# Eight weight slots from the last part of the output projection on, with its adds and the norm's parameter loads reordered

## The chip, the cores and the metric

One core of one Trainium2 chip. The metric is the device time of one execution, in microseconds; a number given for a kernel is the median of several runs. A profiled execution gives the span from the first instruction to the last and the trace that rows are read from.

## The reference

Two post-norm residual layers over an input x of (1, 256, 2048) in float32; each layer is a mixer and an MLP, and each of these ends in a layer norm:

```python
for l in range(DEPTH):                                   # DEPTH = 2
    if l % 2 == 0:   # input projection 2048 -> 6144, conformer convolution + HGRN2 recurrence
        mix = jnp.concatenate([a_out, b_out], axis=-1) @ ev_w_out[j]
    else:            # input projection 2048 -> 6152, forgetting attention + chunked attention
        mix = jnp.concatenate([c_out, d_out], axis=-1) @ od_w_out[j]
    x = layer_norm(ALPHA * x + mix, ln_mix_g[l], ln_mix_b[l])
    h = jnp.square(jax.nn.relu(x @ mlp_w1[l])) @ mlp_w2[l]      # 2048 -> 8192 -> 2048
    x = layer_norm(ALPHA * x + h, ln_mlp_g[l], ln_mlp_b[l])
```

layer_norm subtracts the row's mean, divides by the root of its variance, and multiplies by g and adds b, vectors of 2048. So there are four norms: behind mixer 0, MLP 0, mixer 1 and MLP 1.

## The kernel before, in words

All products are fp32 products made of three fp32r matmuls. Every weight value is split into a high and a low part, and so is every activation: high times high, weight-low times high, weight-high times activation-low (L1303, L1304, L1305).

**Slots.** Weights stream through in chunks of 256 rows by 512 columns, 512 KB each, numbered 0 to 767 over the whole program; the number is called the slot. Layer 0's mixer has slots 0 to 127 (0 to 95 its input projection, 96 to 127 its output projection), MLP 0 has 128 to 383, layer 1's mixer 384 to 511 and MLP 1 512 to 767. For each slot s there are four steps on four engines:

- SP loads the chunk into `raw`, a ring of 4 buffers, once the split of slot s - 4 is done (L314, L341 in the MLP).
- ScalarE copies it rounded into `w_hi` (the split; L476, L702 in the MLP) and increments `hi_ready`.
- VectorE subtracts that from raw into `w_lo` (L788, L1176 in the MLP) and increments `lo_ready`.
- TensorE does 12 matmuls with it, 6 for each half of the 256 rows of x (r = 0 and r = 1), and increments `chunk_used` at the end of r = 1.

`w_hi` and `w_lo` have 4 buffers each in the mixers, and 8 in the MLPs, where the other four (`w_hi2`, `w_lo2`) lie in scratch memory `scr` that the mixers use for their own intermediates. `deep(s)` says where eight are used: slots 128 to 391, and from 512 on. `used_before(s)` is the slot whose buffer s takes, and so the slot that TensorE must be done with before s is split: s - 4 or s - 8. The first four slots of each MLP (128 to 131, 512 to 515) wait for none, since nothing used their buffers.

**Tiles.** A tile is 512 output columns for 256 rows, in one of two PSUM buffers (`gemm0`, `gemm1`); tile t needs the buffer of t - 2 emptied. The output projection goes by three parts of its input (groups of channels as they become ready), each with four tiles; the last part has slots 120 to 127 in layer 0 and 504 to 511 in layer 1, two slots to a tile, tiles 20 to 23. Tile 19 is the last of the part before. VectorE adds each tile to the residual X, once for each half of the rows (`add_row`, L816). For the last part it takes the row statistics at once (`tile_stats`, L831). Where the add of a tile stands among the splits on VectorE is set by `add_before(s)`: ahead of the split of the slot four after the tile's last one. The last two tiles (22, 23) are done rows first: TensorE does r = 0 of slots 124 to 127, then r = 1 of them.

**The norm.** `mix_norm` first runs VectorE's splits up to slot 131 (515), then `layer_norm` with `first_rows`, the adds of tiles 22 and 23 for r = 0, then mean and variance (L840, L842), subtraction of the mean times g (`centre`, L846), a reciprocal root on POOL (`inverse_root`, L404), scaling plus b (`scale`, L852). TensorE transposes the normed pieces (`row_piece`, L1415), the first piece already in the middle of the last slot of tile 23; ScalarE and VectorE make `x_hi` (`row_hi`, L501) and `x_lo` (`row_lo`, L863) of them. `second_rows` are the adds for r = 1. Splits of slots 132 to 139 stand among these steps, by `upto` in `layer_norm` on ScalarE and on VectorE. The norm behind MLP 0 runs by the same function, with only one tile left to add.

**The MLP.** Four blocks of 32 + 32 slots: four tiles with w1, four with w2. After a w1 tile ScalarE does relu (L696) and square (L698, `h_row`), and TensorE transposes the result (`hidden`, L1689) behind the first four half-slots of the next tile. On ScalarE relu and square of tile i stand behind the splits of the first seven slots of the next tile, so for the first tile of an MLP behind those of slots 140, 141 and 142 (524, 525, 526).

**POOL.** It has one stream of instructions. It loads the norm's g and b, each spread to all 128 partitions, into the two rows of `lnp` (`ln_params`, L369), as soon as the last norm's scaling is done, and behind the second such load the constants of the odd layer (`odd_constants`). For the first norm it waits for the transposes of the last recurrence output (`pair_full`, O1) and for `cat_ready`, since `lnp` held the convolution's and the recurrence's rows.

## Time and profile before

| what | value |
|---|---|
| median of 3 runs | 2310.24 us (2310.06 to 2310.41) |
| the profiled execution | 2308.35 us, span 2306.6 us |
| TensorE matmuls busy | 2250.6 us (98%) |
| VectorE busy | 1342.0 us (58%) |
| ScalarE busy | 1056.7 us (46%) |
| POOL busy | 35.8 us (2%) |
| mean granted TensorE clock | 0.991 |
| read from HBM | 414.79 MB, 181 GB/s over the span with what is written |
| each load of a weight chunk / of a row of norm parameters | 512 KB / 1024 KB |

Matmuls are pipelined, so that their busy time overlaps; a stretch in which TensorE waits shows in the waits and in gaps of its timeline, not in the 98%. The granted clock is given as a share of 2.4 GHz. A landing time is from a load's issue to the arrival of its data.

### The profile page before, as it was taken

To read this page: it belongs to the slowest core of one execution; us is meant where nothing else is said; L and a number is where in the kernel's file an instruction comes from. 1 tells how busy PE (TensorE), PEld (TensorE's weight loads), DVE (VectorE), ACT (ScalarE), POOL (GpSimd) and SP (SyncE) were. 2 spreads that over 40 slices of the span, in tenths; PEclk is the share of its full clock that TensorE was granted. 3 is DMA by queue.
4 is the path that set the end of the run, shared out by engine and by line. 5 is a ranking of instruction groups with operands and counts; after the bars stand their busy time and mean duration, and the time that the engine had idled before them with its cause. 6 is when DMAs were issued, how large, how long until landed. Compare 5 with 4: busy or idle time off the path is not lost.

```text
span 2306.6 us, 28499 instructions
## 1 busy us (share of the span) xinstructions
PE 2250.6 (98%) x10331; PEld 1865.2 (81%) x10331; DVE 1342.0 (58%) x1472; ACT 1056.7 (46%) x1146; POOL 35.8 (2%) x68
## 2 busy tenths in 40 slices
PE   8999999889999999999999999998999999999998
PEld 7888788668888888888878888886888888888886
DVE  4898986845544445544565545567454445454455
ACT  4555565344444344344434444444444444543542
POOL 2000000000000000000000000000000000000000
PEclk9999999989999999999999999999999999999999
DMA  7555535575655555655545555565556555556553
GB/s 241 167 161 156 173 128 170 178 225 183 192 191 188 196 183 182 199 193 183 191 163 157 170 177 165 168 192 193 186 186 200 183 197 183 182 193 200 183 188 109
DMA packets 213040, 418.50 MB, mean 181 GB/s; under 512 B 12793, under 2 KB 13361, under 8 KB 211904
## 3 DMA queue, kind: packets, MB, share of 16 engines
q1 hardware_dynamic: 211120, 406.90, 55.0%
q0 software_dynamic: 1808, 10.04, 1.2%
q8 instruction: 78, 1.28, 0.2%
q14 instruction: 34, 0.28, 0.0%
HBM read 414.79 MB, written 2.10 MB: 181 GB/s over the span
## 4 chain that ended last, share of the span: by engine, by line
PE 90%; DVE 5%; DMA 2%; issue 1%; ACT 1%; DVEq 0%; SPq 0%; ACTq 0%
PE gemm L1303 28%; PE gemm L1305 28%; PE gemm L1304 28%; DVE lnp L1047 2%; DMA raw<-in_mlp_w 2%; PE pair L1689 1%; DVE w_lo L788 1%; PE pair L1458 1%; ACT w_hi L476 1%; PE pair L1375 1%; PE pair L1415 1%; DVE X L846 0%; PE pair L1531 0%; PE pair L1603 0%; PE pair L1576 0%
## 5 line engine op out<-in xcount | busy, mean ns | idle before, releaser
L1176 DVE TENSOR_TENSOR w_lo<-raw,w_hi 128x1024 fp32r<-128x1024 f32 x488 | 596.7, 1225 | 491.4 <-ACT w_hi L702 459.7
L702 ACT ACTIVATE w_hi<-raw 128x1024 fp32r<-128x1024 f32 x492 | 522.1, 1061 | 646.5 <-PE gemm L1305 625.2
L1303 PE MATMUL gemm<-w_hi,x_hi 128*128 128x512 f32 x1792 | 711.3, 397 | 7.9 <-DVE w_lo L788 7.6
L1305 PE MATMUL gemm<-w_hi,x_lo 128*128 128x512 f32 x1792 | 701.0, 391 | 0.0
L1304 PE MATMUL gemm<-w_lo,x_hi 128*128 128x512 f32 x1792 | 700.6, 391 | 0.0
L1303 PE MATMUL gemm<-w_hi,c_hi 128*128 128x512 f32 x1280 | 501.2, 392 | 1.0 <-DVE X L813 1.0
L1304 PE MATMUL gemm<-w_lo,c_hi 128*128 128x512 f32 x1280 | 499.0, 390 | 0.0
L1305 PE MATMUL gemm<-w_hi,c_lo 128*128 128x512 f32 x1280 | 499.0, 390 | 0.0
L788 DVE TENSOR_TENSOR w_lo<-raw,w_hi 128x1024 fp32r<-128x1024 f32 x280 | 340.3, 1222 | 205.1 <-ACT w_hi L476 199.6
L476 ACT ACTIVATE w_hi<-raw 128x1024 fp32r<-128x1024 f32 x276 | 289.4, 1056 | 304.6 <-PE gemm L1305 266.1
L1303 PEld LDWEIGHTS gemm<-w_hi,x_hi 128*128 128x128 f32 x1792 | 338.5, 189 | 83.1 <-issue 6.7
L1305 PEld LDWEIGHTS gemm<-w_hi,x_lo 128*128 128x128 f32 x1792 | 338.2, 189 | 71.7
L1304 PEld LDWEIGHTS gemm<-w_lo,x_hi 128*128 128x128 f32 x1792 | 338.7, 189 | 67.0
L1303 PEld LDWEIGHTS gemm<-w_hi,c_hi 128*128 128x128 f32 x1280 | 241.1, 188 | 50.5 <-DVE X L813 1.2
L1305 PEld LDWEIGHTS gemm<-w_hi,c_lo 128*128 128x128 f32 x1280 | 240.9, 188 | 49.9
L1304 PEld LDWEIGHTS gemm<-w_lo,c_hi 128*128 128x128 f32 x1280 | 240.9, 188 | 49.5
L1148 DVE SCALAR_TENSOR_TENSOR X<-X,factor,gemm 128x512 f32<-128x512 f32 x64 | 47.6, 744 | 109.0 <-PE gemm L1305 109.0
L1047 DVE SCALAR_TENSOR_TENSOR lnp<-scr,lnp 128x256 f32<-128x256 f32 x240 | 100.4, 479 | 0.0
L1161 DVE TENSOR_TENSOR c_lo<-pair,c_hi 128x1024 fp32r<-128x1024 f32 x32 | 39.2, 1225 | 92.3 <-ACT c_hi L689 92.2
L689 ACT ACTIVATE c_hi<-pair 128x1024 fp32r<-128x1024 f32 x32 | 32.9, 1027 | 99.0 <-PE pair L1689 99.0
L1689 PE MATMUL pair<-ident,scr 128*128 128x128 f32 x256 | 34.1, 277 | 14.8 <-ACT scr L698 14.8
L1689 PEld LDWEIGHTS pair<-ident,scr 128*128 128x128 f32 x256 | 30.6, 144 | 19.6 <-ACT scr L698 15.6
(194 smaller groups left out, 784.2 us busy)
## 6 DMA issues: line engine op xcount, KB each, us to landing
raw<-in_mlp_w SPq DMA_DIRECT2D x512, 512.0 KB, 4.7
raw<-in_ev_w_in SPq DMA_DIRECT2D x96, 512.0 KB, 3.8
raw<-in_od_w_in SPq DMA_DIRECT2D x96, 512.0 KB, 4.0
raw<-in_ev_w_out SPq DMA_DIRECT2D x32, 512.0 KB, 4.0
raw<-in_od_w_out SPq DMA_DIRECT2D x32, 512.0 KB, 3.6
lnp<-in_ln_mix_g POOLq DMA_DIRECT2D x2, 1024.0 KB, 5.8
lnp<-in_ln_mix_b POOLq DMA_DIRECT2D x2, 1024.0 KB, 8.0
lnp<-in_ln_mlp_g POOLq DMA_DIRECT2D x2, 1024.0 KB, 5.2
```

Of the source, the lines that this page charges most:

```text
L476: act.activation(hi_of_chunk(s), raw[:, s % RING], ACT.Copy).then_inc(hi_ready, 1)
L689: act.activation(c_hi[:, 4 * (i - 1):4 * i, :], quad[0], ACT.Copy).then_inc(h_hi, 1)
L702: act.activation(hi_of_chunk(s), raw[:, s % RING], ACT.Copy).then_inc(hi_ready, 1)
L788: dve.tensor_tensor(lo_of_chunk(s), raw[:, s % RING], hi_of_chunk(s).bitcast(F32), ALU.subtract).then_inc(lo_ready, 1)
L1047: ins = dve.scalar_tensor_tensor(out=cv[:, ch, :], in0=src, scalar=cw[:, ch, j:j + 1], in1=cv[:, ch, :], op0=ALU.mult, op1=ALU.add)
L1148: dve.scalar_tensor_tensor(out=Xj, in0=Xj, scalar=factor[:, bass.ds(b, 1)], in1=gemm[t % 2][:, r, :], op0=ALU.mult, op1=ALU.add).then_inc( ...
L1161: dve.tensor_tensor(c_lo[:, 4 * (i - 1):4 * i, :], quad[0], c_hi[:, 4 * (i - 1):4 * i, :].bitcast(F32), ALU.subtract).then_inc(h_ready, 1)
L1176: dve.tensor_tensor(lo_of_chunk(s), raw[:, s % RING], hi_of_chunk(s).bitcast(F32), ALU.subtract).then_inc(lo_ready, 1)
L1303: pe.matmul(acc[:, r, :], hi[:, k + c, rows], high, start=begin, stop=False)
L1304: pe.matmul(acc[:, r, :], hi[:, k + c, rows], low, start=False, stop=False)
L1305: return pe.matmul(acc[:, r, :], lo[:, k + c, rows], high, start=False, stop=end)
L1689: ins = pe.transpose(quad[0][:, cc, r * P:(r + 1) * P], urow[(i - 1) % 2][:, r, cc * P:(cc + 1) * P], ident[:, :])
```

## The change

- `deep`, `used_before`: eight slots from the first slot of the last part (120 and 504, the new list `DEEP0`) on. The first four of them, whose buffers lie in scratch memory, wait for slot 111 (495) to be done, the end of the mixer's use of that memory (`SCR_FREE`). Slots 128 to 131 (512 to 515) now wait for the slot eight before.
- `add_before`: from tile 19 on an add stands ahead of the split eight after the tile's last slot.
- `second_rows` now has three steps, and `add_row` can leave its statistics to `row_stats`. In VectorE's `layer_norm` the first of them stands ahead of the scaling and the second ahead of the first `row_lo`; the third piece is scaled behind the second `row_lo`.
- ScalarE's `layer_norm`: one more split ahead of the first `row_hi`, and one more ahead of the third.
- POOL: g for the first norm as soon as the convolution is done with its row of `lnp`, b behind O1. Parameters of later norms wait for `h_row` 8 (24) in the second block of the MLP or, for the norm of mixer 1, for `chunk_used` 400; the odd constants for `h_row` 12, in the third block.

TensorE's and SP's instructions keep their order.

```diff
--- before.py
+++ after.py
@@ -95,9 +95,15 @@
 STORES = [(0, 0, 8), (0, 8, 8), (1, 0, 4), (1, 4, 4), (1, 8, 4), (1, 12, 4)]
 
 
+
+
+DEEP0 = [SLOT_MLP[layer] - DEEP for layer in range(DEPTH)]
+SCR_FREE = [SLOT0[layer] + LEVEL_SLOT[1] + 22 for layer in range(DEPTH)]
+
+
 def deep(s):
 
-    return SLOT_MLP[0] <= s < SLOT0[1] + CPT or s >= SLOT_MLP[1]
+    return DEEP0[0] <= s < SLOT0[1] + CPT or s >= DEEP0[1]
 
 
 def slot_of(s):
@@ -106,8 +112,11 @@
 
 def used_before(s):
 
+    for layer in range(DEPTH):
+        if s in range(DEEP0[layer], DEEP0[layer] + RING):
+            return SCR_FREE[layer] - 1
     if deep(s):
-        return None if s in range(SLOT_MLP[0], SLOT_MLP[0] + RING) or s in range(SLOT_MLP[1], SLOT_MLP[1] + RING) else s - DEEP
+        return s - DEEP
     return s - RING if s >= RING else None
 
 
@@ -445,15 +454,23 @@
 
                 pool.tensor_tensor(ss, ss, mhalf[:, 0:8], ALU.pow).then_inc(rstd_ready, 1)
 
+
+            pool.wait_ge(conv_ready, 1)
+            row(lnp[:, 0, :], ln_mix_g[0], D, lnp_loaded)
             pool.wait_ge(pair_full[0], USE[0]["O1"] + 1)
-            pool.wait_ge(cat_ready, 2)
-            ln_params(0)
+            row(lnp[:, 1, :], ln_mix_b[0], D, lnp_loaded)
 
             inverse_root(1)
             for which in range(1, 4):
                 pool.wait_ge(normed, NO * which)
+
+                if which == 2:
+                    pool.wait_ge(chunk_used, SLOT0[1] + 2 * CPT)
+                else:
+                    pool.wait_ge(h_row, FB * NT * (which // 2) + 2 * NT)
                 ln_params(which)
                 if which == 1:
+                    pool.wait_ge(h_row, 3 * NT)
                     odd_constants()
                 inverse_root(1 + which)
 
@@ -504,14 +521,11 @@
             def layer_norm(which, s0, ahead):
 
 
-                upto(s0 + 5)
-                for n in (0, 1, 2):
-                    row_hi(which, n)
                 upto(s0 + 6)
-                row_hi(which, 3)
-                row_hi(which, 4)
+                row_hi(which, 0)
+                row_hi(which, 1)
                 upto(s0 + 7)
-                for n in (5, 6, 7):
+                for n in range(2, 8):
                     row_hi(which, n)
                 upto(s0 + CPT - 1 + min(ahead, 1))
                 row_hi(which, 8)
@@ -799,7 +813,7 @@
                 dve.wait_ge(hi_sem, value)
                 dve.tensor_tensor(lo, quad[p][:, 0:lo.shape[1], :], hi.bitcast(F32), ALU.subtract).then_inc(ready, 1)
 
-            def add_row(layer, part, j, r):
+            def add_row(layer, part, j, r, with_stats=True):
 
                 i = 12 + NT * part + j
                 t = TILE0[layer] + i
@@ -814,16 +828,20 @@
                                              ).then_inc(done, 1)
                 else:
                     dve.tensor_tensor(Xj, tile, Xj, ALU.add).then_inc(done, 1)
-                if part == PARTS - 1:
-                    dve.wait_ge(done, NT * ((PARTS + FB) * layer + part) + j + 1)
-                    tile_stats(j, r)
+                if part == PARTS - 1 and with_stats:
+                    row_stats(layer, j, r)
+
+            def row_stats(layer, j, r):
+                dve.wait_ge((x_sum0, x_sum)[r], NT * ((PARTS + FB) * layer + PARTS - 1) + j + 1)
+                tile_stats(j, r)
 
             def add_before(s):
 
                 for layer in range(DEPTH):
                     for part in range(PARTS):
                         for j in range(NT if part < PARTS - 1 else NT - 2):
-                            if s == SLOT0[layer] + PART_SLOT[part] + PART_CHUNKS[part] * (j + 1) - 1 + RING:
+                            last = SLOT0[layer] + PART_SLOT[part] + PART_CHUNKS[part] * (j + 1) - 1
+                            if s == (last + RING if last + RING < DEEP0[layer] else last + DEEP):
                                 for r in range(RT):
                                     add_row(layer, part, j, r)
 
@@ -870,13 +888,15 @@
                 dve.wait_ge(lnp_loaded, 32 * which)
                 statistics(which, 0, taken)
                 c = [centre(0, *PIECES[i]) for i in range(3)]
+                second_rows[0]()
                 rstd_wait(which, 0)
-                for i in range(3):
-                    scale(0, *PIECES[i], c[i])
+                scale(0, *PIECES[0], c[0])
+                scale(0, *PIECES[1], c[1])
+                second_rows[1]()
                 row_lo(which, 0)
-                second_rows[0]()
                 row_lo(which, 1)
-                second_rows[1]()
+                scale(0, *PIECES[2], c[2])
+                second_rows[2]()
                 row_lo(which, 2)
                 statistics(which, 1, RT * NT)
                 c = [centre(1, *PIECES[i]) for i in range(3)]
@@ -911,8 +931,8 @@
                 rstd_wait(4, 0)
                 for piece, centred in zip(STORES[:2], c):
                     scale(*piece, centred)
-                second_rows[0]()
-                second_rows[1]()
+                for rows in second_rows:
+                    rows()
                 statistics(4, 1, RT * NT)
                 c = [centre(*piece) for piece in STORES[2:]]
                 rstd_wait(4, 1)
@@ -1128,12 +1148,15 @@
             def mix_norm(layer):
                 upto(SLOT_MLP[layer] + RING - 1)
                 x_sums[0] += PARTS * NT
+                part = PARTS - 1
 
                 def first_rows():
-                    add_row(layer, PARTS - 1, NT - 2, 0)
-                    add_row(layer, PARTS - 1, NT - 1, 0)
-
-                second_rows = [lambda: add_row(layer, PARTS - 1, NT - 2, 1), lambda: add_row(layer, PARTS - 1, NT - 1, 1)]
+                    add_row(layer, part, NT - 2, 0)
+                    add_row(layer, part, NT - 1, 0)
+
+                second_rows = [lambda: add_row(layer, part, NT - 2, 1, with_stats=False),
+                               lambda: row_stats(layer, NT - 2, 1),
+                               lambda: add_row(layer, part, NT - 1, 1)]
                 layer_norm(2 * layer + 1, SLOT_MLP[layer], first_rows, second_rows, RT * NT - 2, RING)
 
             def add_block(layer, b, j, r):
@@ -1190,7 +1213,7 @@
                 def first_rows():
                     add_last(layer, NT - 1, 0)
 
-                second_rows = [lambda: None, lambda: add_last(layer, NT - 1, 1)]
+                second_rows = [lambda: None, lambda: None, lambda: add_last(layer, NT - 1, 1)]
                 if layer == 0:
                     upto(SLOT0[1] + RING - 1)
                     layer_norm(2, SLOT0[1], first_rows, second_rows, RT * NT - 1, 0)
```

VectorE from the split of slot 509 to the norm of mixer 1, before (`w_lo2` is the second set of four buffers; `rows_done` counts tiles whose r = 0 is done, `x_sum0` and `x_sum` the adds for r = 0 and r = 1):

```order
L788 TENSOR_TENSOR w_lo<-raw,w_hi 128x1024 [waits chunk_used,raw_full2,hi_ready]
L816 TENSOR_TENSOR X<-gemm1,X 128x512 [waits rows_done]
L831 BN_STATS stats<-X 128x6 [waits x_sum0]
L816 TENSOR_TENSOR X<-gemm1,X 128x512 [waits chunk_used]
L831 BN_STATS stats<-X 128x6 [waits x_sum]
L788 TENSOR_TENSOR w_lo<-raw,w_hi 128x1024 [waits chunk_used,raw_full3,hi_ready]
L788 TENSOR_TENSOR w_lo2<-raw,w_hi2 128x1024 [waits raw_full0,hi_ready]
L788 TENSOR_TENSOR w_lo2<-raw,w_hi2 128x1024 [waits raw_full1,hi_ready]
L788 TENSOR_TENSOR w_lo2<-raw,w_hi2 128x1024 [waits raw_full2,hi_ready]
L788 TENSOR_TENSOR w_lo2<-raw,w_hi2 128x1024 [waits raw_full3,hi_ready]
L816 TENSOR_TENSOR X<-gemm0,X 128x512 [waits rows_done]
L831 BN_STATS stats<-X 128x6 [waits x_sum0]
```

The same stretch now, from the split of slot 510 on:

```order
L802 TENSOR_TENSOR w_lo<-raw,w_hi 128x1024 [waits chunk_used,raw_full2,hi_ready]
L830 TENSOR_TENSOR X<-gemm1,X 128x512 [waits rows_done]
L830 TENSOR_TENSOR X<-gemm1,X 128x512 [waits chunk_used]
L802 TENSOR_TENSOR w_lo<-raw,w_hi 128x1024 [waits chunk_used,raw_full3,hi_ready]
L802 TENSOR_TENSOR w_lo2<-raw,w_hi2 128x1024 [waits chunk_used,raw_full0,hi_ready]
L830 TENSOR_TENSOR X<-gemm0,X 128x512 [waits rows_done]
L849 BN_STATS stats<-X 128x6 [waits x_sum0]
L830 TENSOR_TENSOR X<-gemm0,X 128x512 [waits chunk_used]
L849 BN_STATS stats<-X 128x6 [waits x_sum]
L802 TENSOR_TENSOR w_lo2<-raw,w_hi2 128x1024 [waits chunk_used,raw_full1,hi_ready]
L802 TENSOR_TENSOR w_lo2<-raw,w_hi2 128x1024 [waits chunk_used,raw_full2,hi_ready]
```

The add of tile 19 stands behind the split of 510 instead of 506, that of tile 20 behind 512 and that of tile 21 (not shown) behind 514; the split of 515 then is the only one between it and the adds of tiles 22 and 23.

VectorE at the scaling of the norm of mixer 1, from the add for r = 1 that now stands ahead of it:

```order
L830 TENSOR_TENSOR X<-gemm0,X 128x512 [waits chunk_used]
L870 SCALAR_TENSOR_TENSOR X<-X,rstd,lnp 128x256 [waits dve_link,rstd_ready]
L870 SCALAR_TENSOR_TENSOR X<-X,rstd,lnp 128x256 [waits dve_link]
L849 BN_STATS stats<-X 128x6 [waits x_sum]
L881 TENSOR_TENSOR x_lo<-pair0,x_hi 128x2x128 [waits xt_hi]
L881 TENSOR_TENSOR x_lo<-pair1,x_hi 128x2x128 [waits xt_hi]
L870 SCALAR_TENSOR_TENSOR X<-X,rstd,lnp 128x512 [waits dve_link]
L830 TENSOR_TENSOR X<-gemm1,X 128x512 [waits chunk_used]
```

Before, three scalings stood first, then the first `x_lo`, the add of tile 22 with its statistics, the second `x_lo`, and the add of tile 23.

## Rows read from the trace of the kernel before

**Rows 1.** Who TensorE waited for: total us, times, longest us.
```profile
PE pair L1689 <- ACT scr L698: 14.8, 2, 10.7
PE pair L1415 <- DVE X L852: 11.7, 5, 5.7
```
**Rows 2.** Timeline, TensorE: start us, us, engine, line, operation [idle before <- releaser].
```profile
432.08 0.66 PE L1415 MATMUL pair<-ident,X 128*128 128x128 f32 x2 [5.72 <-DVE X L852]
...
479.49 1.97 PE L1689 MATMUL pair<-ident,scr 128*128 128x128 f32 x8 [10.71 <-ACT scr L698]
...
1165.09 0.38 PE L1415 MATMUL pair<-ident,X 128*128 128x128 f32 x2
...
1189.02 0.30 PE L1415 MATMUL pair<-ident,X 128*128 128x128 f32 x1 [0.35 <-DVE X L852]
...
1569.20 0.66 PE L1415 MATMUL pair<-ident,X 128*128 128x128 f32 x2 [4.84 <-DVE X L852]
...
1594.81 0.30 PE L1415 MATMUL pair<-ident,X 128*128 128x128 f32 x1 [0.39 <-DVE X L852]
...
1609.74 0.33 PE L1689 MATMUL pair<-ident,scr 128*128 128x128 f32 x1 [4.06 <-ACT scr L698]
```
**Rows 3.** Stretches: length, busy us (instructions) of each engine, PEclk, DMA share, GB/s.
```profile
264.00:272.00 8.00, 4.59 (x24) 3.55 (x24) 8.00 (x17) 2.54 (x3) 0.00 (x0) 1.00 0.27 74
...
479.50:485.00 5.50, 5.50 (x18) 4.74 (x19) 2.45 (x2) 2.79 (x3) 0.00 (x0) 0.54 0.80 260
1609.70:1615.00 5.30, 5.26 (x20) 4.34 (x21) 3.06 (x3) 3.02 (x3) 0.00 (x0) 0.68 0.87 281
```
**Rows 4.** Timeline, VectorE, ahead of the norm of mixer 1.
```profile
1556.43 4.62 DVE L788 TENSOR_TENSOR w_lo<-raw,w_hi 128x1024 fp32r<-128x1024 f32 x4
...
1563.92 0.68 DVE L816 TENSOR_TENSOR X<-gemm,X 128x512 f32<-128x512 f32 x1
...
1565.25 0.67 DVE L816 TENSOR_TENSOR X<-gemm,X 128x512 f32<-128x512 f32 x1
...
1568.58 1.54 DVE L852 SCALAR_TENSOR_TENSOR X<-X,rstd,lnp 128x256 f32<-128x256 f32 x3
```
**Rows 5.** Landing times of weight loads (L341) issued from 440 to 458.5.
```profile
DMA to landing us min/median/max: 3.8/4.1/4.3
```
**Rows 6.** Timeline, ScalarE, splits of slots 121, 125 and 126.
```profile
400.78 1.05 ACT L476 ACTIVATE w_hi<-raw 128x1024 fp32r<-128x1024 f32 x1
...
410.82 1.06 ACT L476 ACTIVATE w_hi<-raw 128x1024 fp32r<-128x1024 f32 x1 [1.66 <-PE gemm L1305]
413.54 1.06 ACT L476 ACTIVATE w_hi<-raw 128x1024 fp32r<-128x1024 f32 x1 [1.66 <-PE gemm L1305]
```
**Rows 7.** Timeline, SP's queue: issue of the loads for slots 125 and 526.
```profile
403.31 0.37 SPq L314 DMA_DIRECT2D raw<-in_ev_w_out  x1
...
1599.23 0.37 SPq L341 DMA_DIRECT2D raw<-in_mlp_w  x1
```
**Rows 8.** Landing times of weight loads (L314) issued from 400 to 412.
```profile
DMA to landing us min/median/max: 5.5/6.9/7.3
```
**Rows 9.** Timeline, POOL: first of the two parameter loads, two norms.
```profile
1189.17 0.61 POOL L369 DMA_DIRECT2D lnp<-in_ln_mix_g  x1 [18.13 <-DVE X L852]
...
1594.96 0.58 POOL L369 DMA_DIRECT2D lnp<-in_ln_mlp_g  x1 [18.15 <-DVE X L852]
```
**Rows 10.** Landing times of weight loads (L341) issued from 1596 to 1603.
```profile
DMA to landing us min/median/max: 7.2/7.5/7.9
```
**Rows 11.** Landing times of weight loads (L341) issued from 458.5 to 470.
```profile
DMA to landing us min/median/max: 11.8/13.9/14.3
```
**Rows 12.** Timeline, ScalarE: split of slot 526, then square.
```profile
1606.63 1.06 ACT L702 ACTIVATE w_hi<-raw 128x1024 fp32r<-128x1024 f32 x1 [0.30 <-DMA raw<-in_mlp_w]
...
1608.63 1.06 ACT L698 ACTIVATE scr<-scr 128x1024 f32<-128x1024 f32 x1
```
**Rows 13.** ScalarE's waits for DMA in the MLPs: total us, times, longest us.
```profile
ACT w_hi L702 <- DMA raw<-in_mlp_w: 21.2, 6, 10.4
```

## The prediction

> **What bounds the kernel now.** I read the views from the total down to single rows. The waits of TensorE come first [rows 1]: it idles for 26.5 us at two lines, 14.8 us at the transposes of the hidden rows (L1689) and 11.7 us at the transposes of freshly normed rows (L1415). The timeline of TensorE says where [rows 2]. Four waits make 25.3 us: 5.72 and 4.84 us before the first transposes behind the mixer's norm (432.08 in layer 0, 1569.20 in layer 1), and 10.71 and 4.06 us before the first hidden transposes of each MLP (479.49, 1609.74). The norm behind the first MLP, at 1165.09, waits for nothing, so it is the measure of an undisturbed norm. Everywhere else the matmuls are back to back and nothing on another engine counts.
>
> A wait costs more than itself. The granted clock was 0.54 in 479.5 to 485.0 and 0.68 in 1609.7 to 1615.0 [rows 3], so part of these stretches ran at 1.2 GHz instead of 2.4 after TensorE had idled 10.71 and 4.06 us: (1 - 0.54) x 5.5 = 2.5 us and (1 - 0.68) x 5.3 = 1.7 us lost. Behind the norms the loss is read from lengths: from first to last front transposes the undisturbed norm takes 1189.02 - 1165.09 = 23.93 us, layer 1's takes 1594.81 - 1569.20 = 25.61 us: 1.7 us lost; I take 1.7 for layer 0 too. In 264 to 272, with 8.00 - 4.59 = 3.41 us of idleness in it, the clock stayed at 1.00 [rows 3]: shorter waits lose none. All four places together hold 25.3 + 7.6 = 32.9 us.
>
> **Wait 1, the mixer's norm.** What ends last is VectorE. In layer 1 it did four splits from 1556.43 (the next MLP's first slots), the last of them late, and began the adds of the last tiles at 1563.92 [rows 4], when TensorE had long finished the first rows of these tiles. From the add at 1565.25 to TensorE's restart at 1569.20 are 3.95 us. Layer 0 has the same order.
>
> With eight slots from the last part on, splits 120 to 131 no longer wait for the slot four back but for the one eight back, so the four splits stand ahead of the adds in time, not behind. Costs on VectorE: a split 4.62 / 4 = 1.15 us, an add with its statistics 1565.25 - 1563.92 = 1.33, both halves 2.66.
>
> Layer 1: ScalarE's splits there waited for TensorE, not for DMA. Loads land in 3.8 to 4.3 us when quiet [rows 5], and a buffer of four comes round in 4.1 + 1.06 + 1.15 plus hand-overs, 6.5 us, 1.6 per slot against 2.72 per slot of TensorE (from one released split to the next) [rows 6]. Starting with split 504, VectorE gains about 1.1 us per slot and reaches the add of tile 19 (now behind split 510) some 2 us before TensorE asks for it. The last four slots run as 5.44 us of first rows, then second rows. First rows of the last tile end 4.7 us before 1564.4, at 1559.7; VectorE is through split 515 and the add before by then. From there 3.95 + 0.65 (the add of the second rows, put in ahead of the scaling) gives 1564.3: TensorE stands there at 1564.36. Wait gone, clock kept; of the new order behind it, 0.3 us may show since the statistics come ahead of the first x_lo. Gain 4.84 + 1.7 - 0.3 = **6.2**.
>
> Layer 0: the ramp starts later, since ScalarE is held by the c_hi copy until its split 121 at 400.78 [rows 6]. The load for slot 125 went out at 403.31 [rows 7] and does so again. Loads between 400 and 412 landed in 5.5 to 7.3 us beside 2 MB of norm parameters [rows 8]; 1 MB of these is now earlier, so I take 5, and 3.8 and 7.3 as ends. Slot 125 lands at 408.3, 126 by 409.5, split 126 ends at 411.6, and the add of tile 19, which stands behind it now, ends at 412.9. TensorE wants tile 21's buffer at 410.8 (the end of slot 121, which released the split at 410.82): **a new wait of 2.1 us** (ends 0.9 and 4.4). What is queued on VectorE behind it: splits 127 to 131 (5 x 1.13 back to back), two tiles' adds (5.3), the first add of the last tiles (1.33), then 4.6: 16.9 us, restart at 429.8. TensorE's own work from 412.9 is 5.44 + 5.44 + 4.7 = 15.6, so it waits again, 1.3 us. Restart 429.8 against 432.08 is 2.3, plus the clock 1.7: **4.0**.
>
> **Wait 2, the first hidden transposes.** The norm parameters leave POOL's queue at 1594.96 [rows 9], just when SP starts on the slots that the norm held back [rows 7]. Between 1596 and 1603 these landed in 7.2 to 7.9 us [rows 10]; in layer 0, where odd-layer constants followed, in 11.8 to 14.3 [rows 11], against 3.8 to 4.3 just before [rows 5]. The square that TensorE waits for stands on ScalarE behind three of these splits: split 1606.63, square ending 3.1 us later [rows 12]. With the parameters gone, the third load, issued at 1599.23, lands at about 4.5 us, 1603.8, and the square is done at 1606.9; TensorE wants it at 1609.74 - 4.06 = 1605.68. **1.2 us stay** (4.1 to 4.9 us of landing give 0.8 to 1.6), short enough to keep the clock. Layer 1 gains 4.06 - 1.2 + 1.7 = **4.5**, layer 0 10.71 - 1.2 + 2.5 = **12.0**.
>
> DMA: Bandwidth & Descriptors of the Trainium skill, section Issuing engines are not separate DMA queues, says that transfers issued from different engines run on the same DMA engines and interleave. By that rule, the trace agrees that POOL's loads delay SP's [rows 10, 11]. It also speaks against the change: bytes moved to another moment still interleave with weight loads there, and the sum would lose what they cost at the new place.
>
> **What moving the loads costs.** 2 MB go into the second block of each MLP, the constants into the third block of the first, 2 MB into layer 1 at slot 400, 1 MB to about 387 us. In the MLP, ScalarE waited for DMA at L702 six times, 21.2 us [rows 13], and all six lie behind the two mixer norms: in the middle it never did. A load issued there has four slots (10.9 us) less 2.3 us of splitting, 8.6, before ScalarE is late, and four more slots before TensorE is. 7.9 us fits, 14.3 is covered by the eight slots. At slot 400 only four slots exist: 8.6 us before ScalarE, some 14 before TensorE; 7.9 fits too, and 2 MB issued at 1189.17 [rows 9], some ten slots earlier, cost TensorE no wait. So 0, with bounds of 0 and 3. If that cover is gone, the price is Wait 2's, 12 us at worst.
>
> SP's order is unchanged; POOL's waits have only its own reciprocal roots behind them, which come due hundreds of us later. ScalarE's split 134 ahead of the first x_hi needs the slot done half a chunk before: 0 to 0.3. The norm at 1165 changes its order and has no wait to lose: 0 (bounds -0.3 and 0.3). The last norm is as before.
>
> **Sum.** 6.2 + 4.0 + 12.0 + 4.5 = 26.7 us off the profiled execution, 2308.35 (span 2306.6), which stands 1.9 below the median of the runs, 2310.24. So 2281.7 there, **2283.5** for the median. Bounds: all four waits and clock losses gone, 32.9: 2277.3. Least: layer 0's norm 1, layer 1's 4.5, the hidden waits 9.5 and 2.5, mid-stage -3: 14.5, 2295.7.
>
> **The rivals.**
> - *The hidden waits are the four raw buffers', not the parameters'.* Then layer 0 falls only to what layer 1 has, 4.06 + 1.7, a gain of 7.4, and layer 1 keeps its own. For: even by my sum the third load is late. Against: 7.2 to 7.9 us of landing. 10.2 + 7.4 = 17.6: 2292.6. Chance 0.12.
> - *VectorE stays the chain at the norm*: the ramp never gets ahead, as nearly in layer 0, and new waits eat the old. Only 16.5: 2293.7. Chance 0.11. In layer 0 alone: 2287.5, part of my range.
> - *The loads starve TensorE at their new places.* They share the DMA engines with the weight loads there too, and each of the three places costs what layer 0's now does [rows 2, 3], 10.71 + 2.5 = 13.2 us, 39.6 in all against 26.7 gained: 2323.1, slower. It decides from 8.9 us apiece; it needs landings beyond 14 us at all three. Against: no such wait in mid-stage now [rows 13]. Chance 0.02; a partial loss that ends between 2295 and 2305, 0.04.
> - *The change does not do what it says*: the eight slots wait for slot 111 at their start. It ended some 22 us before slot 120 begins (eight slots of 2.72), so it holds nobody. 2310, chance 0.02.
>
> **How the numbers follow.** My forecast has 0.69 and its own range is 2278 to 2290. Taking in the first two rivals leaves out under 0.2: 2277.5 to 2294. A measurement of this kernel tells 0.2% (4.6 us) from no change. Faster needs under 2305.6: 0.95; same 0.02; slower 0.03.
>
> **What would show it.** In the profile after: at the mixer norms L1415 waits under 0.5 us in layer 1 and 1 to 2 in layer 0, with a new wait of about 2 us for an add at about 411; L1689 waits about 1 us twice; ScalarE waits under 5 us for DMA at L702's successor in total; the granted clock stays 1.00 behind all four. Wrong if a hidden wait above 3 us stays, if TensorE idles at mid-MLP or near slot 400, or if the norm of layer 1 still waits over 2 us.

## The result, and the profile of the changed kernel

The changed kernel takes **2287.07 us** (median; 2285.41 to 2289.18) against 2310.32 for the kernel before, run beside it: a ratio of 0.9899, 95% interval 0.9882 to 0.9916. The forecast was 2283.5 in a range of 2277.5 to 2294.0. The profiled execution took 2288.11, a little over its median; before it was 2308.35, a little under, so the two profiles differ by 20.2 us and the medians by 23.2.

Who TensorE waited for, after: total us, times, longest us. These answer to [rows 1].
```profile
PE gemm L1326 <- DVE w_lo L802: 6.5, 8, 3.4
...
PE gemm L1326 <- DVE X L830: 3.4, 1, 3.4
PE pair L1712 <- ACT scr L712: 2.8, 2, 1.6
...
PE pair L1438 <- DVE X L870: 1.9, 4, 0.9
```
The transposes of normed rows (L1415 before, L1438 now) wait 1.9 us instead of 11.7, those of the hidden rows (L1689, now L1712) 2.8 instead of 14.8. One line is new: a matmul waits 3.4 us for an add. The first line holds waits for VectorE's splits, nearly all far from the change; the longest of them stands at 264 us, as before.

Timeline of TensorE after, the places that answer to [rows 2]; start us, us, engine, line, operation [idle before <- releaser].
```profile
414.92 0.79 PE L1326 MATMUL gemm<-w_hi,c_hi 128*128 128x512 f32 x1 [3.44 <-DVE X L830]
...
469.98 1.09 PE L1712 MATMUL pair<-ident,scr 128*128 128x128 f32 x8 [1.62 <-ACT scr L712]
...
1554.92 0.41 PE L1438 MATMUL pair<-ident,X 128*128 128x128 f32 x2 [0.85 <-DVE X L870]
...
1591.12 1.09 PE L1712 MATMUL pair<-ident,scr 128*128 128x128 f32 x8 [1.18 <-ACT scr L712]
```
Four waits again, but of 7.1 us instead of 25.3. The norm of layer 0 is not among them: nothing over 0.25 us is left ahead of its first transposes. In its place stands the new wait at 414.92, in front of slot 122, for the add of tile 19.

Stretches after, answering to [rows 3]: length, busy us (instructions) of PE, PEld, DVE, ACT, POOL, then the granted clock, DMA share, GB/s.
```profile
264.00:272.00 8.00, 4.63 (x13) 3.39 (x12) 8.00 (x18) 2.34 (x2) 0.00 (x0) 0.69 0.24 72
...
415.00:420.50 5.50, 5.50 (x13) 4.34 (x14) 5.43 (x7) 1.06 (x2) 0.00 (x0) 0.50 0.83 259
469.90:475.00 5.10, 5.02 (x26) 4.32 (x27) 3.67 (x3) 4.12 (x5) 0.00 (x0) 1.00 0.78 233
1273.00:1276.00 3.00, 3.00 (x10) 2.29 (x10) 0.00 (x0) 0.00 (x0) 0.00 (x0) 0.66 0.67 180
...
1554.90:1560.00 5.10, 5.03 (x24) 3.45 (x24) 4.46 (x9) 2.31 (x4) 0.00 (x0) 1.00 0.00 0
1591.00:1596.00 5.00, 4.88 (x26) 4.17 (x27) 3.65 (x3) 4.03 (x5) 0.00 (x0) 1.00 0.82 267
```
Behind the waits of 0.85 to 1.62 us the clock stays at 1.00, 2.4 GHz, in this profile. Behind the new wait it is 0.50, 1.2 GHz: the twelve matmuls of slot 122 take from 414.92 to the first of slot 123 at 420.21, 5.29 us for 2.72, so 2.6 us are lost beside the 3.44. The same happened in two places that the change does not touch: behind the wait at 264 (1.00 before, 0.69 now), and at 1274, where TensorE had not waited at all.

**Where the 20.2 us came from.** I took for each slot the start of its first matmul in the two profiles and noted how the difference steps. The mixer norm of layer 0, from slot 121 to slot 129, gave 1.15 us (old wait and clock gone, new wait and clock in); the hidden transposes behind it 11.5; the norm of layer 1 5.3; the hidden transposes of layer 1 4.5. That is 22.4. The other 2.2 went in code that the change does not touch: 1.4 by the clock at 1274 and 0.8 elsewhere, most of it behind the wait at 264, where the clock took 2.6 us and some 2 came back up to 306, where waits of the kernel before did not come. What is left is 20.2.

Layer 0's ramp after: ScalarE's splits of slots 125 to 127 (408.28, 411.35, 412.64), then VectorE with the splits of 125 and 126 and the two adds of tile 19.
```profile
408.28 1.06 ACT L493 ACTIVATE w_hi<-raw 128x1024 fp32r<-128x1024 f32 x1 [2.84 <-DMA raw<-in_ev_w_out]
411.35 1.06 ACT L493 ACTIVATE w_hi<-raw 128x1024 fp32r<-128x1024 f32 x1 [2.01 <-DMA raw<-in_ev_w_out]
412.64 1.06 ACT L493 ACTIVATE w_hi<-raw 128x1024 fp32r<-128x1024 f32 x1 [0.23 <-DMA raw<-in_ev_w_out]
```
```profile
409.37 1.23 DVE L802 TENSOR_TENSOR w_lo<-raw,w_hi 128x1024 fp32r<-128x1024 f32 x1 [1.92 <-ACT w_hi L493]
412.44 1.23 DVE L802 TENSOR_TENSOR w_lo<-raw,w_hi 128x1024 fp32r<-128x1024 f32 x1 [1.84 <-ACT w_hi L493]
413.58 1.28 DVE L830 TENSOR_TENSOR X<-gemm,X 128x512 f32<-128x512 f32 x2
```
In [rows 6] these splits waited for TensorE; now they wait for DMA: the load of slot 126 is what is late. TensorE wanted tile 21's buffer at 411.48, and the add that frees it could only follow split 126.

Landing times of weight loads after: issued 404 to 406.5; 460 to 472, behind layer 0's norm; 1570 to 1584, behind layer 1's. These answer to [rows 8], [rows 11] and [rows 10].
```profile
DMA to landing us min/median/max: 4.2/6.1/6.3
```
```profile
DMA to landing us min/median/max: 4.2/4.6/5.1
```
```profile
DMA to landing us min/median/max: 3.7/3.9/4.5
```
The loads ahead of the hidden transposes land in 4.6 us instead of 13.9, and in 3.9 instead of 7.5. Those of the ramp are better than before, but not quiet.

### The profile page after: what moved, and what is told of

Its sections match the earlier page's. It is cut to its first block, busy times and chain, and to the rows that moved or that the text cites. A ratio compares the mean times of both kernels' runs of the same rounds, so it can differ in the third digit from the quotient of the medians.

```text
span 2286.4 us, 28509 instructions
## 1 busy us (share of the span) xinstructions
PE 2249.9 (98%) x10331; PEld 1864.2 (82%) x10331; DVE 1341.9 (59%) x1472; ACT 1057.0 (46%) x1146; POOL 36.6 (2%) x68
## 3 DMA queue, kind: packets, MB, share of 16 engines
q8 instruction: 78, 1.28, 0.2%
## 4 chain that ended last, share of the span: by engine, by line
PE 91%; DVE 4%; DMA 2%; ACT 1%; issue 1%; DVEq 0%; SPq 0%; ACTq 0%
PE gemm L1326 29%; PE gemm L1328 29%; PE gemm L1327 29%; PE pair L1712 1%; DVE w_lo L802 1%; DVE lnp L1067 1%; DMA raw<-in_mlp_w 1%; PE pair L1481 1%; ACT w_hi L493 1%; PE pair L1398 1%; PE pair L1438 0%; PE pair L1554 0%; PE pair L1626 0%; PE pair L1599 0%; DVE X L864 0%
## 5 line engine op out<-in xcount | busy, mean ns | idle before, releaser
L710 ACT ACTIVATE scr<-gemm 128x1024 f32<-128x1024 f32 x32 | 32.9, 1028 | 8.1 <-PE gemm L1328 8.1
L1712 PEld LDWEIGHTS pair<-ident,scr 128*128 128x128 f32 x256 | 29.9, 141 | 7.6 <-ACT scr L712 3.6
```

Source lines behind the costliest of these rows:

```text
L1712: ins = pe.transpose(quad[0][:, cc, r * P:(r + 1) * P], urow[(i - 1) % 2][:, r, cc * P:(cc + 1) * P], ident[:, :])
```

## The experiments

**The theory to test.** The hidden waits went because the parameters left the DMA engines there; the loads cost nothing in mid-stage; what missed the forecast is one wait in layer 0, for the add of tile 19 behind a late load, and the clock behind it. **Rivals:** the ring of eight did most of it and the loads little; the loads at 387 and 401 us are themselves what delays the ramp; the new order inside the norms is what remains; and the extra loads in mid-stage take a little everywhere.

**1. The loads alone** (the kernel before with this edit and no other).
```diff
+            pool.wait_ge(conv_ready, 1)
+            row(lnp[:, 0, :], ln_mix_g[0], D, lnp_loaded)
...
-            pool.wait_ge(cat_ready, 2)
-            ln_params(0)
+            row(lnp[:, 1, :], ln_mix_b[0], D, lnp_loaded)
...
+                if which == 2:
+                    pool.wait_ge(chunk_used, SLOT0[1] + 2 * CPT)
+                else:
+                    pool.wait_ge(h_row, FB * NT * (which // 2) + 2 * NT)
...
+                    pool.wait_ge(h_row, 3 * NT)
```


> The kernel before with POOL's part of the change alone (parameter loads and constants in mid-stage). If the hidden waits were the parameters' and mid-stage is free, the two waits at the hidden transposes fall from 10.7 and 4.1 us to about 1.6 and 1.2, their clock loss goes, and the time falls by 15 to 17 us, to 2293 to 2296; both norm waits (5.7 and 4.8 us) stay. If the four raw buffers made the waits, 4 us stay at each and the gain is under 10 us. If the loads cost something at their new places, TensorE shows a wait in mid-MLP or near slot 400.

Measured 2293.25 us, ratio 0.993 (0.9913 to 0.9946): 16.4 us of the change's 23.2. Its four waits on TensorE:
```profile
431.15 0.42 PE L1422 MATMUL pair<-ident,X 128*128 128x128 f32 x2 [5.02 <-DVE X L859]
...
468.57 1.09 PE L1696 MATMUL pair<-ident,scr 128*128 128x128 f32 x8 [1.28 <-ACT scr L705]
...
1555.85 0.66 PE L1422 MATMUL pair<-ident,X 128*128 128x128 f32 x2 [4.80 <-DVE X L859]
...
1595.06 1.71 PE L1696 MATMUL pair<-ident,scr 128*128 128x128 f32 x8 [2.14 <-ACT scr L705]
```
The hidden waits fall from 10.71 and 4.06 to 1.28 and 2.14, and the norm waits stay. `raw` still has four buffers here, and the eight slots begin where they did. So most of the hidden waits was the parameters', which settles the first rival of the prediction.

**2. The ring and the order alone** (the changed kernel with the old place of POOL's loads, the edit of run 1 undone).

> The changed kernel with POOL's loads as before. If norms and loads are separate, the norm of layer 1 gains the same 5 to 6 us, and the hidden waits are back at 10 and 4 us. With 2 MB of parameters from 400 us on again, the loads for slots 125 and 126 land a us or two later than after the change, so the new wait for the add of tile 19 grows from 3.4 to 5 us or more and layer 0's norm loses. Time 2302 to 2306. If that wait has nothing to do with the parameters, it stays at 3.4 us.

Measured 2308.38 us, ratio 0.9996 (0.9986 to 1.0006): nothing gained that can be told from noise, and worse than expected. TensorE's waits, and the DMA page of the stretch 403 to 406.8 (queue: packets, MB, share of 16 engines; then KB and median us to landing):
```profile
417.11 0.79 PE L1319 MATMUL gemm<-w_hi,c_hi 128*128 128x512 f32 x1 [6.53 <-DVE X L823]
...
480.96 1.97 PE L1705 MATMUL pair<-ident,scr 128*128 128x128 f32 x8 [11.16 <-ACT scr L705]
...
1608.05 1.97 PE L1705 MATMUL pair<-ident,scr 128*128 128x128 f32 x8 [4.53 <-ACT scr L705]
```
```profile
q0 software_dynamic: 193, 1.43, 96.2%
...
raw<-in_ev_w_out SPq DMA_DIRECT2D x3, 512.0 KB, 9.2
```
With both parameter loads (POOL's queue, q0) in flight, the ramp's weight loads land in 9.2 us and the add of tile 19 is 6.53 us late, against 3.44. In layer 1, where no parameters are loaded in the ramp, the norm waits 1.14 us with 0.93 us for an add ahead of it, against 4.84 before, so the eight slots do gain there. The hidden waits and layer 0 ate it. By the medians the two halves are not additive: 16.4 and 1.2 us alone, 23.2 together. In layer 0 the eight slots need the loads gone from the ramp.

**3. The add of tile 19 two slots ahead, in both layers** (the changed kernel with this add before the split of 125 and 509, not behind 126 and 510).
```diff
-                            if s == (last + RING if last + RING < DEEP0[layer] else last + DEEP):
+                            if s == (last + RING if last + RING < DEEP0[layer] else last + DEEP - 2 * (part < PARTS - 1)):
```


> The changed kernel with the add of tile 19 two splits earlier (ahead of the split of slot 125 and 509). VectorE stood idle there for 1.9 us in layer 0. If the new wait is the order of VectorE, the 3.4 us at 411 and the low clock behind it (2.6 us) go, but VectorE's chain of splits and adds then ends later than TensorE, and a wait of 2 to 3.5 us comes back ahead of the first transposes at 427 to 430; net 3 us less than after the change. In layer 1 nothing changes. If the wait at 411 is the late loads themselves, it stays as a wait for the split of slot 122 or later.

Measured 2284.92 us, ratio 0.9901 (0.9884 to 0.9918). Its waits from 411 us to the norm of layer 0:
```profile
421.08 0.50 PE L1326 MATMUL gemm<-w_hi,c_hi 128*128 128x512 f32 x1 [1.87 <-DVE X L830]
429.99 0.41 PE L1438 MATMUL pair<-ident,X 128*128 128x128 f32 x2 [1.14 <-DVE X L870]
```
The wait of 3.44 is gone with its clock loss. Two come in its place further on, the second of them the one that the prediction had put there (1.3 us). Slot by slot this profile is 3 to 4 us ahead of the changed kernel's behind layer 0's norm; the medians show 2.2 of it, but the ratios to the kernel before, 0.9901 here and 0.9899 there, show nothing. So run 3 shows what made the wait, and not a gain in time.

**4. The second mixer parameter held until slot 121 is done.**
```diff
+            pool.wait_ge(chunk_used, SLOT_MLP[0] - 6)
             row(lnp[:, 1, :], ln_mix_b[0], D, lnp_loaded)
```


> The changed kernel with the load of b for the first norm held until slot 121 is done (411 us instead of 401). If that 1 MB delays the loads for slots 125 and 126, they land in about 4 us instead of 5 to 6, the split of 126 ends 2 us earlier and the wait for the add of tile 19 falls from 3.4 to about 1.5 us, with the clock kept: 4 us less in layer 0. If the loads were slow for another reason, the wait stays at 3.4.

Measured 2285.51 us, ratio 0.9898 (0.9881 to 0.9914). The wait, the landing of the loads issued from 403 to 406 (POOL's load now leaves at 411.15), and stretches of the ramp, columns as above:
```profile
414.20 0.63 PE L1327 MATMUL gemm<-w_hi,c_hi 128*128 128x512 f32 x1 [3.62 <-DVE X L831]
```
```profile
DMA to landing us min/median/max: 4.1/6.3/6.5
```
```profile
407.00:409.00 2.00, 2.00 (x10) 1.66 (x9) 0.60 (x1) 1.06 (x1) 0.00 (x0) 1.00 0.89 305
409.00:411.00 2.00, 1.58 (x7) 0.96 (x6) 0.62 (x1) 0.36 (x1) 0.00 (x0) 1.00 0.95 347
```
The wait stays, so the parameter is not its cause. The first of four loads issued 1.1 to 1.4 us apart lands in 4.1 us, the others in 6.3 to 6.5 (the fourth, in 6.4, is a load of the MLP and not in this view), with the DMA engines busy for 0.89 to 0.95 of the time. That fits loads that delay each other; no run spaced them out to show it. The quiet 3.8 to 4.3 us of [rows 5] were read where loads go out a slot apart. The clock was not kept behind this wait either: 0.70 in 414.3 to 420.

**5. As run 3, with relu and square one split earlier** in each MLP's first tile.
```diff
-                    if i < NT and c == CPT - 1:
+                    if i < NT and c == (CPT - 2 if i == 0 and CPT not in splits and RING in splits and 0 not in splits else CPT - 1):
```


> The kernel with the earlier add (e3) and, for the first tile of each MLP, relu and square one split earlier on ScalarE (ahead of slots 142 and 526, not behind). If the rest of the hidden waits (1.7 and 1.4 us) is the third weight load that relu stands behind, both vanish and nothing else moves: 3 us less than e3, about 2282. If ScalarE's split then comes too late for TensorE, a wait for w_lo takes their place.

Measured **2281.21 us**, ratio 0.9875 (0.986 to 0.989). No hidden wait over 0.25 us is left in layer 0, and 0.29 in layer 1. So the rest of the hidden waits was the third split that stood ahead of the square. The gain over run 3 and over the changed kernel is at the edge of the noise (the changed kernel's interval began at 0.9882); runs 10 and 11 come back to it.

**6. The old order inside the norms**, all else as changed.
```diff
+                upto(s0 + 5)
+                for n in (0, 1, 2):
+                    row_hi(which, n)
...
-                second_rows[0]()
                 rstd_wait(which, 0)
-                scale(0, *PIECES[0], c[0])
-                scale(0, *PIECES[1], c[1])
-                second_rows[1]()
+                for i in range(3):
+                    scale(0, *PIECES[i], c[i])
                 row_lo(which, 0)
+                second_rows[0]()
...
```


> The changed kernel with VectorE's and ScalarE's order inside the norms as before the change. The add for r = 1 no longer stands between the subtraction and the scaling, so TensorE restarts 0.65 us sooner at the norm of layer 1 (its wait of 0.85 us falls to 0.2 or so); behind it the adds and statistics delay the second and third x_lo, for which I expect new waits of 0.5 to 1.5 us in the first two slots. Net between -0.5 and +1.5 us per mixer norm: if the reorder was worth anything the time rises, by 2 us at most; the norm behind MLP 0 does not move.

Measured 2285.21 us, ratio 0.989 (0.9875 to 0.9906), the changed kernel's own within the intervals. Layer 1's norm waits 0.52 us here, where 0.2 was expected, and 0.85 in the changed kernel (1.14 in run 11). The reorder inside the norms neither gains nor costs anything that shows.

**7. As run 3, with the split of 131 and 515 put behind the third scaling**, since VectorE is a us late at the norms.
```diff
+                upto(s0 + RING - 1)
...
-                upto(SLOT_MLP[layer] + RING - 1)
+                upto(SLOT_MLP[layer] + RING - 2)
```
(The adds of tiles 21 move with it, to just ahead of those of the last two tiles.)

> e3 with the split of slot 131 (515) moved from ahead of the last tiles' adds to behind the third scaling of the norm, so that VectorE's chain up to TensorE's restart is 1.15 us shorter. If this chain alone sets the restart, the waits of 1.1 us at both mixer norms vanish (2.2 us less than e3). If VectorE is as full behind the restart, the same 1.15 us comes back as a wait for x_lo or for the split itself within the first four slots, and the time stays.

Measured 2299.24 us, ratio 0.9949 (0.9935 to 0.9962): worse than run 3 by 11 us by the ratios, 14 by the medians. TensorE's new wait in layer 1, and ScalarE and SP's queue ahead of it:
```profile
1566.99 0.80 PE L1329 MATMUL gemm<-w_hi,x_hi 128*128 128x512 f32 x1 [5.29 <-DVE x_lo L881]
```
```profile
1564.67 1.06 ACT L493 ACTIVATE w_hi<-raw 128x1024 fp32r<-128x1024 f32 x1 [6.25 <-DMA raw<-in_mlp_w]
1565.64 0.58 ACT L518 ACTIVATE x_hi<-pair 128x512 fp32r<-128x512 f32 x1
```
```profile
1560.83 0.37 SPq L350 DMA_DIRECT2D raw<-in_mlp_w  x1
```
The norm waits fell to 0.4 us and less, and 5.1 and 5.3 us came instead, in layer 0 and in layer 1, with the clock at 0.61 in 1567 to 1572. A raw buffer is free for the next load only when VectorE has split it. The late split sent the load of 519 out at 1560.83, and ScalarE stood for it with the third `x_hi` behind. Run 9 tests this.

**8. Every later pair of parameters loaded twice**, 6 MB more over the three later norms, all at the new places.
```diff
+                pool.wait_ge(lnp_loaded, 64 * which)
+                row(lnp[:, 0, :], g, D, lnp_loaded)
+                row(lnp[:, 1, :], b, D, lnp_loaded)
```


> The changed kernel with each later pair of parameter loads done twice, one pair after the other, at the new places: 6 MB more (2 in each MLP's second block, 2 at slot 400). If loads in mid-stage are free, no new wait of TensorE and the same time within 2 us. If they cost what they cost behind the norms (about 1.8 us per MB), 10 us more; at slot 400, where four slots are the cover, a wait would show first.

Measured 2287.71 us, ratio 0.99 (0.9885 to 0.9915), against 0.9899 of the changed kernel. In 713 to 735 us, around the doubled pair (first) and the single one (changed kernel, second):
```profile
713.00:735.00 22.00, 22.00 (x103) 18.32 (x102) 10.53 (x10) 9.58 (x10) 2.15 (x4) 1.00 0.93 355
```
```profile
713.00:735.00 22.00, 22.00 (x103) 18.31 (x102) 12.65 (x12) 10.08 (x10) 1.10 (x2) 1.00 0.78 278
```
TensorE is busy for all 22 us in both, with the DMA engines at 0.93 instead of 0.78. It is so too at the place behind slot 400, in 1214 to 1240 us, where they are at 0.84 instead of 0.68. Mid-stage had room for twice the bytes, one pair behind the other.

**9 to 11, on one chip together: run 7 mended, run 5 again, the changed kernel again.** Run 9 is run 7 with run 5's relu, and ScalarE's third `x_hi` ahead of the split of 135 and 519:
```diff
-                row_hi(which, 0)
-                row_hi(which, 1)
+                for n in range(5):
+                    row_hi(which, n)
                 upto(s0 + 7)
-                for n in range(2, 8):
+                for n in (5, 6, 7):
```


> The version with the earlier adds and relu, and VectorE's split of tile 131/515 behind the third scaling; ScalarE now writes its third piece of the normalised rows before its split of 135/519 instead of behind it. If the 5.1 and 5.3 us waits of the run before with that split moved came from ScalarE standing in front of its piece for the load of 135/519, they vanish here; the waits of about 1 us ahead of the mixer norms go too, and about 1 us comes back as a wait for the last x_lo or the late split: 2279.5 to 2283, within 2 us of the version with the earlier adds and relu alone. If instead VectorE's chain behind the moved split is what was late, the waits for x_lo stay at 4 to 5 us in both layers: 2292 to 2297.

> The version with the add of tile 19/23 ahead of split 125/509 and relu and square one split earlier, again, beside the changed kernel itself on the same chip: 2279.5 to 2283.5. If its 4 us or so under the changed kernel are real they recur (the two differ by 3.5 to 6 us here); if they were the luck of which clock losses fell into which executions, the two come out within 2 us.

> The changed kernel unchanged, in another profile: 2284 to 2289. The waits recur to a tenth or two of a us: about 3.4 us for the add of tile 19 in layer 0, 1.6 and 1.2 us for the squares, 0.9 us ahead of layer 1's norm. What may differ is the granted clock behind the 3.4 us waits at 264 and 411, and the low clock at 1274 without a wait: if that is a property of the code it is back at the same matmuls, if it is the execution's own it is gone or elsewhere.

| kernel | median us | ratio to before | 95% interval |
|---|---|---|---|
| 9: run 7 mended, with run 5's relu | 2282.38 | 0.9882 | 0.9866 to 0.9899 |
| 10: run 5 again | 2283.20 | 0.9889 | 0.9873 to 0.9906 |
| 11: changed kernel again | 2287.15 | 0.9904 | 0.9887 to 0.9920 |

Before was 2308.76 here. In run 9 the 5 us waits vanish, so ScalarE's place in line was the cause of run 7's loss; 0.94 us for `x_lo` comes back in each layer, as the first theory had it. Moving the split is worth 0.8 us against run 10, less than can be told apart. Run 5's version is 4.0 us under the changed kernel, after 5.9 the first time. The intervals overlap, but each of its four executions here (2281.59 to 2284.55) is below each of the changed kernel's (2286.65 to 2291.47). Run 11's waits and stretches:
```profile
PE pair L1712 <- ACT scr L712: 4.2, 2, 2.3
PE gemm L1326 <- DVE X L830: 3.9, 1, 3.9
```
```profile
268.00:274.00 6.00, 6.00 (x32) 5.04 (x31) 6.00 (x13) 1.97 (x2) 0.00 (x0) 1.00 0.58 175
...
415.00:420.50 5.50, 5.50 (x16) 4.20 (x15) 5.42 (x7) 1.50 (x2) 0.00 (x0) 0.56 0.85 276
...
470.00:475.00 5.00, 4.91 (x19) 4.06 (x20) 2.45 (x3) 3.07 (x4) 0.00 (x0) 0.66 0.66 188
...
1276.00:1280.00 4.00, 4.00 (x19) 3.29 (x18) 1.02 (x1) 1.06 (x1) 0.00 (x0) 1.00 0.36 121
```
My expectation that the waits recur to a tenth or two was too tight: the add is 3.9 us late instead of 3.4, the squares 2.3 and 1.9 instead of 1.6 and 1.2. The clock loss at 415 recurs. Those at 268 and at 1274 do not (the same matmuls stand at 1276 here): they belong to the execution. Two are new. Behind the hidden waits, which were longer this time, the clock was 0.66 in layer 0 and 0.67 in layer 1 (1592.9 to 1598): 1.7 us lost at each, where the first profile of the same kernel lost none.

## Why the prediction was nearly right, step by step

**The verdict and the size.** 2287.07 lies 3.6 us above the forecast and inside its range, and none of the prediction's signs of being wrong came. Of what it said would show, though, the waits at both norms, the size of the new wait, ScalarE's waits for DMA and the clock behind the new wait came out otherwise. It is also near its rival for layer 0 alone, 2287.5, in which new waits eat the old ones there. The profile shows most of that rival: layer 0's norm gained 1.15 us, not 4.0 and not 0. That the two numbers agree to half a us is luck. The sum had 26.7 us for the profile; its four stages gave 22.4 and unchanged code took 2.2 back. The median moved by 23.2, nearer to the sum than the 20.2 of the two profiles, since the profile before was below its median and the one after above.

**Wait 2, layer 0: 12.0 forecast, 11.5 measured; layer 1: 4.5 and 4.5.** The step held in this profile: the waits that stay are 1.62 and 1.18 us where 1.2 was forecast for both, and the clock was kept behind them. Run 1 shows the cause apart from the ring. "Short enough to keep the clock" did not hold in run 11, where 2.29 and 1.93 us stayed and cost 1.7 us of clock each. DMA: Bandwidth & Descriptors of the Trainium skill, section Issuing engines are not separate DMA queues, has the transfers of different engines interleave on the same DMA engines; by that rule the trace agrees again, since in run 2 the packets of POOL's queue took 96.2% of the time of the 16 DMA engines and SP's loads took 9.2 us.

**Moving loads costs 0.** It held; run 8 shows room for as much again. The rival that the loads starve TensorE there is excluded at twice their bytes. ScalarE's forecast wait for DMA (under 5 us) was wrong, and harmless:
```profile
ACT w_hi L716 <- DMA raw<-in_mlp_w: 22.8, 11, 5.8
```
There were 21.2 us in six waits before [rows 13]. ScalarE waits for loads elsewhere now, and one of those waits, of 3.01 us, stands at 725 us behind the moved pair, but TensorE is eight slots away from it.

**Wait 1, layer 1: 6.2 forecast, 5.3 measured.** The clock was kept and the wait fell from 4.84 to 0.85, not to nothing. The step that failed is "VectorE is through split 515 and the add before by then". VectorE, after:
```profile
1539.22 1.23 DVE L802 TENSOR_TENSOR w_lo<-raw,w_hi 128x1024 fp32r<-128x1024 f32 x1 [0.93 <-ACT w_hi L493]
...
1547.92 1.21 DVE L802 TENSOR_TENSOR w_lo<-raw,w_hi 128x1024 fp32r<-128x1024 f32 x1
...
1550.37 0.67 DVE L830 TENSOR_TENSOR X<-gemm,X 128x512 f32<-128x512 f32 x1
```
It worked back to back from 1539.22, and began the last first-rows add at 1550.37. TensorE wanted its rows at 1554.07, 4.7 us before which is 1549.4: a us late. From there to the restart at 1554.92 are 4.55 us, where the sum had 3.95 + 0.65 = 4.60. So the length of the chain was right and its start was not. Most of the us is the 0.93 that VectorE stood idle ahead of the split of 512, which ScalarE began 1.58 us late, for want of the load. The sum gave the loads of this ramp the quiet 3.8 to 4.3 us; those issued from 1521.8 to 1538.5 took 3.5 to 5.7. No run took that idle time away.

**Wait 1, layer 0: 4.0 forecast, 1.15 measured.** Two terms of this sum were wrong. The new wait was right in its place and its releaser, but mis-sized: 3.44 us instead of 2.1. The term at fault is "I take 5" for the landing in the ramp; the first load took 4.2, the next ones 6.1 to 6.3. Run 4 shows that the parameter did not delay them; that they delay each other is a reading of its trace. So landing in the ramp is the term that was too small in both layers. The second term is the clock. The prediction said that waits up to 3.41 us lose none, from one stretch of one execution [rows 3]. Behind the wait of 3.44 us, 2.6 us were lost. The forecast second wait, 1.3 us at the norm, did not come in this profile: by the prediction's own lengths VectorE's chain ends 16.9 us behind the add, at 431.8, and TensorE asks for it 15.6 + 2.6 us behind, at 433.1, so TensorE at half clock gave VectorE the time. With the first wait taken out (run 3) it appeared, at 1.14.

That step was also refutable from the trace of before. It holds a wait of 1.60 us at 343, and the stretch behind it reads:
```profile
346.00:350.00 4.00, 4.00 (x15) 3.20 (x14) 1.85 (x3) 3.07 (x4) 0.00 (x0) 0.75 0.40 133
```
So the clock had fallen already behind a wait half as long, with a group of 16 small transposes between, and I had looked at one stretch that suited the sum.

**Clock loss in unchanged code: 0 forecast, 2.2 in the profile.** No term stood for it. Run 11 shows it to be chance, so it explains the profiled execution (2288.11) more than the median. At 264 the loss is even the common case: of the 13 profiles of all kernels here three kept 1.00 in 264 to 272 (before, run 9, run 11), and the other ten had 0.67 to 0.82. The profile before, from which the sum was read, was one of the lucky ones.

**The reorder, 0 to 0.3:** nothing measurable in run 6.

## What to carry to other kernels

A deeper ring gains only what its loads can deliver: when it starts, several loads go out together and most take longer than one alone, so size the ramp by loads in a burst, and put no work that TensorE waits for behind the last of them. Parameters are best loaded where TensorE has slots in hand and not in the stretch where a stage's first weights are fetched. A load's buffer is freed by the last engine that reads it, so before a split is moved back, look at who stands in front of the load that it frees.

## What the runs showed of the hardware that I had not expected

*The clock behind a wait is not a function of its length alone.* Behind the wait at 264 us, of 3.4 us in every profile, the granted clock in 264 to 272 was 1.00 before [rows 3], in run 9 and in run 11, and 0.69 in the changed kernel's first profile, in the same code. Behind shorter waits it fell as well in some places: in run 1, whose wait for the square was 2.14 us,
```profile
1596.40:1599.00 2.60, 2.60 (x9) 2.06 (x8) 1.95 (x2) 1.02 (x1) 0.00 (x0) 0.54 0.62 191
```
and in run 9 behind 1.89 us (0.76 in 420 to 426), while in run 10 1.68 us in the same place kept it (and so did 1.89 us in runs 5 and 7):
```profile
420.00:426.00 6.00, 4.33 (x13) 3.40 (x14) 4.88 (x7) 0.62 (x1) 0.00 (x0) 0.76 0.55 183
```
```profile
420.00:426.00 6.00, 4.32 (x20) 3.20 (x18) 5.93 (x8) 1.06 (x1) 0.00 (x0) 1.00 0.76 253
```
The loss of 1.4 us at 1274 came with no wait before it. In these profiles waits from 1.6 to 3.4 us thus sometimes cost the clock, 1 to 3 us more, and sometimes did not; what decides in a single case stays open. The six waits of 3.44 to 6.53 us for the add of tile 19 in layer 0 all lost it: 0.50 to 0.70 in the 5 to 6 us behind them.

*Loads in a burst land late.* In run 4, four loads of 512 KB 1.1 to 1.4 us apart landed in 4.1 us (the first) and 6.3 to 6.5 (the rest), with no other queue's load in flight. In run 11 the first three of this ramp took 5.9 to 6.7 us, behind POOL's 1 MB. Which limit of the DMA engines or of HBM sets this was not tried.
